# A hybrid attention, GLA and SwiGLU layer on one core: the order of GLA, merge, norm and FFN work changed

## The reference

```python
h = rmsnorm(x, norm_mix_pre)
(a_q, a_kc, ..., mg) = split(h @ w_in)
o_a = nsa_mixer(...)    # compressed, selected and window attention, 8 heads
o_b = gla_mixer(...)    # gated linear attention, 4 heads
o_c = moba_mixer(...)   # block attention, 8 heads
g = sigmoid(mg).reshape(b, s, 3, D_MODEL)
merged = g[:, :, 0] * (o_a @ w_branch_a) + g[:, :, 1] * (o_b @ w_branch_b) + g[:, :, 2] * (o_c @ w_branch_c)
x = x + rmsnorm(merged @ w_out, norm_mix_post)
h = rmsnorm(x, norm_ffn_pre)
gate, up = split(h @ w_ffn_in)
x = x + rmsnorm((silu(gate) * up) @ w_ffn_out, norm_ffn_post)
```

## Time and profile before

| | us |
|---|---|
| three executions | 1012.82, 1013.41, 1020.36 |
| median | 1013.41 |
| the profiled execution | 1015.79 |
| its span, first to last instruction | 1014.1 |
| TensorE busy in the span | 962.9 |
| mean granted TensorE clock | 0.977 |

### The profile page before, as it was taken

One profiled execution on the slowest core, in us unless ns is written; L12 is line 12 of the kernel. 1 busy time (PEld: TensorE's weight loads), 2 busy tenths in 40 slices (PEclk: granted clock), 3 DMA queues, 4 the chain that ended last, 5 costly groups with the idle time before them and its releaser, 6 DMA issues.

```text
span 1014.1 us, 13017 instructions
## 1 busy us (share of the span) xinstructions
PE 962.9 (95%) x4708; PEld 803.2 (79%) x4708; DVE 461.1 (45%) x863; ACT 404.0 (40%) x724; POOL 196.8 (19%) x182
## 2 busy tenths in 40 slices
PE   5999989989899999999989998999999999899994
PEld 3787878878688788788868887988888888788883
DVE  6246655250445555556657747422222222233335
ACT  4333434332446565667754435222222222223322
POOL 4333233333223243234420001000000000000001
PEclk9899979999989999999989999999999999999998
DMA  5178214422232322355365533122332222222312
GB/s 222 64 113 175 75 63 125 146 83 79 78 110 68 104 75 92 105 169 190 110 241 198 171 128 103 42 79 87 103 100 86 103 98 88 83 95 91 103 62 83
DMA packets 37883, 111.37 MB, mean 110 GB/s; under 512 B 4100, under 2 KB 8644, under 8 KB 37324
## 3 DMA queue, kind: packets, MB, share of 16 engines
q1 hardware_dynamic: 37692, 110.49, 33.9%
q10 hardware_dynamic: 144, 0.26, 0.1%
HBM read 93.93 MB, written 13.66 MB: 106 GB/s over the span
## 4 chain that ended last, share of the span: by engine, by line
PE 87%; DVE 5%; DMA 3%; ACT 2%; issue 2%; POOL 1%; POOLq 0%; SPq 0%; ACTq 0%; DVEq 0%
PE bank L1499 25%; PE bank L1500 24%; PE bank L1501 24%; DMA w_raw<-wpack 3%; PE bank L599 3%; PE bank L591 2%; PE bank L613 1%; PE bank L590 1%; PE bank L611 1%; ACT w_hi L841 1%; PE bank L617 1%; PE bank L1515 1%; PE bank L1648 1%; PE bank L1535 1%; DMA xs<-x_in 1%
## 5 line engine op out<-in xcount | busy, mean ns | idle before, releaser
L1499 PE MATMUL bank<-h_hi,w_lo 128*128 128x512 f32 (+1 forms) x680 | 271.1, 399 | 4.4 <-DVE cqs L1228 3.0
L1500 PE MATMUL bank<-h_lo,w_hi 128*128 128x512 f32 (+1 forms) x680 | 266.8, 392 | 0.0
L1501 PE MATMUL bank<-h_hi,w_hi 128*128 128x512 f32 (+1 forms) x680 | 266.7, 392 | 0.0
L1499 PEld LDWEIGHTS bank<-h_hi,w_lo 128*128 128x128 f32 (+1 forms) x680 | 128.6, 189 | 36.9 <-issue 11.4
L841 ACT ACTIVATE w_hi<-w_raw 128x1024 fp32r<-128x1024 f32 (+1 forms) x85 | 89.3, 1051 | 160.4 <-PE bank L1501 152.1
L1501 PEld LDWEIGHTS bank<-h_hi,w_hi 128*128 128x128 f32 (+1 forms) x680 | 128.3, 189 | 28.2
L1500 PEld LDWEIGHTS bank<-h_lo,w_hi 128*128 128x128 f32 (+1 forms) x680 | 128.8, 189 | 23.8
L777 POOL TENSOR_TENSOR w_lo<-w_raw,w_hi 128x1024 fp32r<-128x1024 f32 (+1 forms) x37 | 88.3, 2388 | 153.1 <-ACT w_hi L841 153.1
L1031 ACT ACTIVATE w_hi<-w_raw 128x1024 fp32r<-128x1024 f32 x40 | 42.5, 1063 | 168.8 <-PE bank L1501 168.8
L784 POOL TENSOR_TENSOR sc<-sc,ast 128x512 f32<-128x512 f32 (+1 forms) x96 | 66.3, 722 | 145.0 <-DVE ast L531 111.1
L1441 DVE TENSOR_TENSOR w_lo<-w_raw,w_hi 128x1024 fp32r<-128x1024 f32 x40 | 49.0, 1226 | 90.9 <-ACT w_hi L1031 90.9
(11 more groups left out here) (276 smaller groups left out, 1559.8 us busy)
## 6 DMA issues: line engine op xcount, KB each, us to landing
w_raw<-wpack SPq DMA_DIRECT2D x146, 512.0 KB, 3.3
gate_logits<-gl_out SPq DMA_DIRECT2D x24, 256.0 KB, 2.1
gl_in<-gate_logits SPq DMA_DIRECT2D x24, 256.0 KB, 3.5
near_bias<-near SPq DMA_DIRECT2D x1, 3072.0 KB, 33.8
xs<-x_in SPq DMA_DIRECT2D x4, 512.0 KB, 5.8
fullb<-near_bias SPq DMA_DIRECT2D x16, 128.0 KB, 2.6
ckx<-cks SPq DMA_DIRECT2D x16, 128.0 KB, 2.4
ob<-gla_out SPq DMA_DIRECT2D x2, 1024.0 KB, 7.1
```

The source lines that it names most:

```text
L1499: mm(out, ll, rh, start=start, stop=False, skip_group_check=True)
L1500: mm(out, lh, rl, start=False, stop=False, skip_group_check=True)
L1501: return mm(out, lh, rh, start=False, stop=stop, skip_group_check=True)
```

## The change

- Start: the gate transposes move behind chunk 2, z behind chunk 1, bT behind 3, the levels behind 5 to 11 and the diagonal behind 12. TensorE goes from chunk 0 straight to chunk 1.
- GLA: kd, qb and a state of three tiles get their own memory. Keys and queries are decayed at chunks 5 to 9, the states made at 10 to 12 in banks 4 and 5, the outputs at 13 to 16 in banks 0 to 3. POOL clears the state.
- The compressed softmax is cut in two; its second half comes on VectorE after the next chunk's eviction.
- Attention: TensorE's wait for the last two ck evictions moves from ahead of step 0 to step 8.
- Merge: products are reordered (`PRODUCTS`: branches a and b of n = 0 to 2 first, then their c), use six banks, and the first four are done in halves in steps 96 to 103. Weight splits run one chunk further ahead. A third mrg buffer.
- Output projection: its wait for all 24 products stands ahead of the third tile of its first chunk.
- Norms: VectorE multiplies by the norm weight as it reads PSUM (`weighted`, `z_weight`), before the rstd is there; one fused pass then scales and adds. `transposed_lo(0)` and `(1)` now stand behind `residual(2)` and `(3)`.
- FFN: the first two activation splits come within the last two tiles of the up stage; the down stage starts with the halves in banks 4 to 7. At the end `z_full` counts halves, and the last tile is stored in two halves, the second from ScalarE's queue.

The core of the diff:

```diff
+PRODUCTS = ([(0, 0), (0, 1), (1, 0), (1, 1), (2, 0), (2, 1), (0, 2), (1, 2), (2, 2)]
+            + [(n, b) for n in range(3, KD) for b in range(3)])
+PRODUCT_BANKS = (0, 1, 6, 7, 2, 3)
+ADDS_BEFORE = [sum(b > 0 for _, b in PRODUCTS[:s]) for s in range(N_GATES)]
...
-AUX = (["gates", "z0", "z1", "bT0", "bT1"] + [f"lv{l}_{t}" for l in range(7) for t in range(2)] + ["lv7"]
-       + ["kd0", "kd1", "o0", "s0", "o1", "s1", "o2", "s2", "o3", "cmp", "cbias"])
+AUX = (["z0", "z1", "gates", "bT0", "bT1"] + [f"lv{l}_{t}" for l in range(7) for t in range(2)]
+       + ["lv7", "cmp", "cbias"])
+C_O = STRAIGHT.index(("kc", 0))
...
-        state = at(204, "state", [P, 2, 256])
+        kd = at(112, "kd", [P, 1024])
+        qb = at(116, "qb", [P, 1024])
+        state = at(120, "state", [P, 3, 2, 256])
...
@@ -451,12 +461,13 @@
                     if n < 7:
                         sa.wait_ge(s_full, head_units(n + 1)[1] + 1)
                     sa.activation(hi_, part, ACT.Copy).then_inc(head_hi, 1)
-                if u % 4 == 1 and 0 <= u // 4 - 1 < N_GATES:
+                if u % 4 == 1 and 0 <= u // 4 - 1 < N_GATES + 2:
                     f = u // 4 - 1
-                    sa.wait_ge(w_used, C_GATE + f + 1)
-                    if f >= 2:
-                        sa.wait_ge(gl_stored[f % 2], 16 * (f // 2))
-                    sa.activation(gl_out[:, f % 2, :], gate_bank(f)[:, :], ACT.Copy).then_inc(gl_copied, 1)
+                    if f < N_GATES:
+                        sa.wait_ge(w_used, C_GATE + f + 1)
+                        if f >= 2:
+                            sa.wait_ge(gl_stored[f % 2], 16 * (f // 2))
+                        sa.activation(gl_out[:, f % 2, :], gate_bank(f)[:, :], ACT.Copy).then_inc(gl_copied, 1)
                     hi(C_GATE + f + 2)
 
         def transposed_lo(ve, t):
...
+
+        def compressed_probs(ve, link):
+
...
+        def branch_part(te, three, s, ks):
+
+            b = PRODUCTS[s][1]
+            c, part, out = C_BR + s // 2, s % 2, bank[PRODUCT_BANKS[s % 6]]
+            xh, xl = [(oa[:, :, 0, :], oa[:, :, 1, :]), (ob2[:, 0, :, :], ob2[:, 1, :, :]),
+                      (oc[:, :, 0, :], oc[:, :, 1, :])][b]
+            if ks[0] == 0:
+                if part == 0:
+                    te.wait_ge(w_hi, c + 1)
+                    lo_split(te, c)
+                if s == 0:
+                    te.wait_ge(head_lo, 8)
+                if s == 1:
+                    te.wait_ge(ob_back, 32)
+                if s < 2:
+                    te.wait_ge(s_max, len(UNITS) - 1 + s)
+                elif s < 4:
+                    te.wait_ge(gl_copied, N_GATES - 3 + s)
+                elif s < 6:
+                    te.wait_ge(t_lo, len(UNITS))
+                else:
+                    te.wait_ge(d_free, s - 5)
+                if s == 6:
+                    te.wait_ge(head_lo, 16)
+            for k in ks:
+                cols = slice(512 * part + k * P, 512 * part + k * P + P)
+                last = three(out[:, :], wh[:, c % 2, cols], wl[:, c % 2, cols], xh[:, k, :], xl[:, k, :],
+                             k == 0, k == 3)
+            if ks[-1] == 3:
+                last.then_inc(p_full if part == 0 else w_used, 1)
...
-            single_out(te, slot_of("ck", 3))
-            single_out(te, slot_of("ck", 2))
...
+                    if v == 0:
+                        single_out(te, slot_of("ck", 3))
+                        single_out(te, slot_of("ck", 2))
...
+                elif u < len(UNITS) + PV_LAG:
+                    s, half = divmod(u - len(UNITS), 2)
+                    branch_part(te, three, s, (2 * half, 2 * half + 1))
...
-            def load_logits(f):
-                if f >= 4:
-                    sp.wait_ge(d_sig, f - 3)
-                sp.dma_start(gl_in[:, f % 4, :], gate_dram[f, :, :]).then_inc(gl_read[f % 4], 16)
+            def load_logits(s):
+                n, b = PRODUCTS[s]
+                if s >= 4:
+                    sp.wait_ge(d_sig, s - 3)
+                sp.dma_start(gl_in[:, s % 4, :], gate_dram[3 * n + b, :, :]).then_inc(gl_read[s % 4], 16)
...
+                if c == 6:
+
+                    sa.wait_ge(kd_sub, 1)
+                    sa.activation(kd[:, :], kd[:, :], ACT.Exp).then_inc(kd_sub, 1)
+                    sa.activation(qb[:, :], bT[:, :], ACT.Exp).then_inc(kd_sub, 1)
                     sa.activation(ebl[:, :], bT[:, :].rearrange("p (n c) -> p n c", c=P)[:, :, P - 1],
-                                  ACT.Exp).then_inc(ex_ready, 1)
...
+                if c == 5:
+                    b3 = bT[:, :].rearrange("p (n c) -> p n c", c=P)
+                    ve.tensor_tensor(kd[:, :].rearrange("p (n c) -> p n c", c=P),
+                                     b3[:, :, P - 1:P].broadcast_to([P, 8, P]), b3, ALU.subtract).then_inc(kd_sub, 1)
+                if c == 7:
+                    ve.wait_ge(kd_sub, 4)
+                    ve.tensor_tensor(kd[:, :], kd[:, :], gk[:, :], ALU.mult).then_inc(kd_ready, 1)
+                if c == 8:
+                    ve.tensor_tensor(qb[:, :], qb[:, :], gq[:, :], ALU.mult).then_inc(kd_ready, 1)
+                if c == 11:
...
+                if 10 <= c < 13:
+                    t = c - 10
+                    ve.wait_ge(st_full, t + 1)
+                    ve.wait_ge(const_ready, 5)
+                    ps_s = bank[4 + t % 2][:, :].rearrange("p (a n) -> p a n", a=2)
...
-                if s % 2 == 0 and s > 0:
-                    hi(C_BR + s // 2 + 1)
+                if s % 2 == 0 and s >= 4:
+                    hi(C_BR + s // 2 + 2)
...
-                sa.wait_ge(z_full, t + 1)
                 for half in range(2):
+                    sa.wait_ge(z_full, 2 * t + half + 1)
                     if t + half > 0:
                         sa.wait_ge(z_sq, 2 * t + half)
                     sa.activation(junk[:, :], bank[4 * half + t][:, :], ACT.Square,
                                   accum_out=stat[:, 56 + 2 * t + half:57 + 2 * t + half]).then_inc(z_sq, 1)
+            sa.wait_ge(out_ready, NT + 1)
+            sa.dma_start(out_d[0, (NT - 1) * P:NT * P, 512:1024], x1[:, NT - 1, 512:1024]).then_inc(stored, 16)
...
+            def weighted(t, half):
+                ve.wait_ge(y_sq, 2 * t + half + 1)
+                cols = slice(512 * half, 512 * half + 512)
+                ve.tensor_tensor(x1[:, t, cols], bank[4 * (1 - half) + t][:, :], wpost[:, cols], ALU.mult).then_inc(y_weighted, 1)
+
             def residual(t):
 
                 ve.wait_ge(y_rstd, t + 1)
-                for half in range(2):
-                    ins = ve.scalar_tensor_tensor(out=x1[:, t, 512 * half:512 * half + 512],
-                                                  in0=bank[4 * (1 - half) + t][:, :], scalar=stat[:, 8 + t:9 + t],
-                                                  in1=wpost[:, 512 * half:512 * half + 512], op0=ALU.mult,
-                                                  op1=ALU.mult)
-                link(ins)
-                ve.tensor_tensor(x1[:, t, :], x1[:, t, :], xr[:, t, :], ALU.add).then_inc(x1_ready, 1)
+                ve.wait_ge(y_weighted, 2 * t + 2)
+                ve.scalar_tensor_tensor(out=x1[:, t, :], in0=x1[:, t, :], scalar=stat[:, 8 + t:9 + t],
+                                        in1=xr[:, t, :], op0=ALU.mult, op1=ALU.add).then_inc(x1_ready, 1)
...
-            for t in range(2):
+            weighted(0, 0)
+            for t in range(NT):
                 y_mean(t)
+                weighted(t, 1)
                 residual(t)
-                lo(C_FIN + 2 + t)
+                if t < 2:
+                    lo(C_FIN + 2 + t)
+                else:
+                    transposed_lo(ve, t - 2)
                 x_mean(t)
+                if t + 1 < NT:
+                    weighted(t + 1, 0)
                 normalised(t)
-            transposed_lo(ve, 0)
-            y_mean(2)
-            residual(2)
-            transposed_lo(ve, 1)
-            x_mean(2)
-            normalised(2)
-            y_mean(3)
-            residual(3)
             lo(C_FIN + 4)
-            x_mean(3)
-            normalised(3)
             transposed_lo(ve, 2)
             transposed_lo(ve, 3)
             lo(C_FIN + 5)
@@ -1433,7 +1489,7 @@
                 ve.wait_ge(w_used, C_FIN + 2 * f + 2)
                 ve.tensor_tensor(act[:, f, :], silu[:, f, :], bank[4 * f + 1][:, :], ALU.mult).then_inc(f_free, 1)
 
...
+            for f in range(NF - 2, NF):
+                hi(C_FIN + 2 * f + 2)
+                act_hi(f - NF + 2)
+                sa.wait_ge(w_used, C_FIN + 2 * f + 1)
+                sa.wait_ge(f_free, f + 1)
+                sa.activation(silu[:, f % 2, :], bank[2 * (f % 2)][:, :], ACT.Silu).then_inc(f_sig, 1)
+                hi(C_FIN + 2 * f + 3)
+            for k in range(2, 4):
...
+            def z_weight(t, half):
+                ve.wait_ge(z_sq, 2 * t + half + 1)
+                cols = slice(512 * half, 512 * half + 512)
```

(54 more changed lines are left out.)

297 lines of the change are left out of this document (142 added, 155 removed).

## The result

The changed kernel took 989.46 us (median of four runs, 986.35 to 993.73), the kernel before 1013.29 beside it: ratio 0.9727, interval [0.9681, 0.9774]. A second measurement on another chip gave 990.5 against 1018.29, ratio 0.9748 [0.9712, 0.9785]. The prediction was 985.4, range 975 to 998, with 0.93 on faster by over 1%. The profiled execution is the one of 986.35 us, span 984.6, where the working gave 987.8.

The account below looks back on a forecast made before the run. TensorE, busy 95% of the span, was taken to bound the kernel through its written order: work, stops and half clock. Gains and losses summed to 28.0 us, from 1015.79 to 987.8, or 985.4 against the median; range 975 to 998.

Parts of the forecast that it names:

- Gates (A): Kernel start: the 2.46 us stop for ScalarE's first copy and 3.15 of slow clock go, 0.6 charged; +5.0 us.
- The stop at 95 us: TensorE's wait for a w_raw transfer queued behind the 3 MB bias table, then splits and products; 0.5 left, +1.9 us.
- GLA (B): GLA stretch: stops of 3.0 (zz) and 1.22 us (gr) and 6.4 of slow clock go; +10.6 us, bounds 4.2 to 10.6.
- Compressed softmax: VectorE evicts the cq chunk before waiting for the exponential, so TensorE's stop there goes; +3.0 us.
- Start of attention (D): The 3.66 us wait for ck evictions becomes 2.15 at step 2, 1.5 charged for clock; +2.9 us, bounds 1.0 to 4.4.
- End of attention, merge (E): Stops of 3.7 and 3.25 of clock go; new 4.1 us stop at chunk C_BR+4, 2.0 for clock; net +0.9 us.
- End of merge: First output chunk's third tile waits for all products, with VectorE's split and products behind the last; -1.9 us, bound 0.
- Residual (F): Residual loop: h_lo pieces come later, stop 5.4 us in place of 2.14, 1.7 of clock as before; -2.8, bounds +1.5, -4.5.
- Up to down (G): FFN, up to down stage: early activation splits remove the as_lo stop, 3.2 plus 1.3 us of clock; +4.5 us.
- Last w_lo: FFN down stage: the 3.03 us stop for the last w_lo stays untouched, as both last chunks are waited for together.
- Tail: VectorE's work after TensorE ends at 1007.4 instead of 1011.03, last transfer 0.3 less; +3.9 us, 0.9 lower by another reading.
- six of nine cases: Clock rule: a TensorE stop costs itself and, in six of nine cases, 1.3 to 3.3 us more at half clock.

Follow-up runs that it names:

- p1: Kernel before with only the change's first part (head of the weight stream, early exponentials, GLA states and outputs in own banks): ratio 0.9848.
- u1: Changed kernel with four repairs to its order, but VectorE's compressed softmax in one call again: 977.76 us, ratio 0.9599 to the kernel before.
- e5: Changed kernel with four repairs to its order, plus the second compression layer's two products one weight chunk later: 972.51 us, ratio 0.9551 to the kernel before.
- e2: Changed kernel, its first output projection chunk waiting only for the product that last had each of banks 6 and 7: 985.52 us, ratio 0.9702.
- e1: Changed kernel with residual input and two norm rows issued between the weight chunks of branch products 2 to 7, not as one block: 985.89 us, 0.9684.
- p3: Kernel before with only the change's third part, the FFN and the norms: ratio 0.9947.

## Why the prediction was right

The mechanism held: the written order of TensorE is the time, and every stop that was to go went. Sizes were off in several steps, most in the clock. What each step was worth, from the profiled execution of before to that of after:

- **Gates (A)**, predicted +5.0: stop 2.46 and slow stretch 3.15 gone, the charged 0.6 at the first level came as 0.48 (0.28 became 0.76). 5.1. Right.
- **The stop at 95 us**, predicted +1.9: mis-sized. 0.5 was to be left, 1.42 was. TensorE was there at 92.4 and not at 92.9, and its operand came at 93.8, behind the 92.5 to 93.6 that were given. From ScalarE's split to the last product it took 5.5 us before and after, so the chain was right and the times of arrival were off. Gain 1.0.
- **GLA (B)**, predicted +10.6: the zz and gr rows are gone and the window 130 to 148 reads 1.00. With the two slow stretches read apart that is 3.0 + 1.22 + 6.8 = 11.0. p1's 1.52% (15.5 us) stands against 17.1 for these first three, but its own profile lost 6.2 us in slow stretches that the changed kernel's doesn't have, so this agreement proves little.
- **Compressed softmax**, predicted +3.0: cqs gone; u1 brought back 3.0 plus clock.
- **Start of attention (D)**, predicted +2.9: the stop was 2.14 at step 2, as worked out (2.15). Of the 1.5 charged for the clock nothing was lost in the profiled execution, so 1.5 + 2.9 = 4.4, the upper bound. e5's execution lost 4.72 x 0.34 = 1.6 behind the very same stop, so the charge was a fair mean.
- **End of attention, merge (E)**, predicted +0.9: the new stop stands where it was put, at 3.06 instead of 4.1. TensorE came at +12.4 (predicted +12.3) after the last P.V product, the logits at +12.5 instead of +13.5. The over-sized term is the landing, taken from the burst of before. Net 3.74 + 3.25 - 3.06 - 1.7 = 2.2.
- **End of merge**, predicted -1.9: 1.89, and e2 shows that it was a wait for product 24 where 21 would do.
- **Residual (F)**, predicted -2.8: the stop is 4.73, below the 5.4, but the clock term failed. "1.7 of clock as before" became 2.9 (in e1's execution, behind the same 4.73 us, 6.71 x 0.23 = 1.5). Net 2.14 + 0.41 - 4.73 + 1.7 - 2.9 = -3.4.
- **Up to down (G)**, predicted +4.5: the as_lo row and its stretch are gone. Right.
- **Last w_lo**: the prediction left it at nothing. The stop stayed at 3.03, but the clock fell behind it this time: 1.7. Not foreseen.
- **Tail**, predicted +3.9: 4.3. POOL's power took 0.55 for all four tiles, once right beside the weighting, here in the changed kernel:

```profile
979.59 0.68 DVE L1543 TENSOR_TENSOR xn<-bank,wfpost 128x512 f32<-128x512 f32 x1
```

```profile
979.75 0.55 POOL L879 TENSOR_TENSOR stat<-stat,minus_half 128x1 f32<-128x1 f32 x1 [2.16 <-DVE stat L1537]
```

Neither was held up. In the kernel before, the power of 1.46 us at 1006.74 lay over an add with both inputs in SBUF:

```profile
1006.57 1.21 DVE L1490 TENSOR_TENSOR x<-x,xn 128x1024 f32<-128x1024 f32 x1
```

That is the case for which the prediction quoted the Trainium skill, "SBUF — State Buffer" (SBUF: two separate sides): the lock is between a GpSimd operation that reads SBUF and a VectorE operation with two inputs from SBUF. The trace agrees, by these few rows alone.

These sum to 5.1 + 1.0 + 11.0 + 3.0 + 4.4 + 2.2 - 1.9 - 3.4 + 4.5 - 1.7 + 4.3 = 28.5 against 28.0 predicted and 29.5 between the spans. The misses are of both signs and cancel, which is luck in the sum. So is some of the early third. The prediction read its stops and slow stretches off one execution of before; p3 has the same code up to 590 us, and in its execution the stop at 95 us was 6.05 and not 2.43, with 6.08 x 0.46 = 2.8 us lost behind it (100 to 107.5) where the profile before lost nothing. The prediction's rule for the clock was miscounted too: its "six of nine cases" with "1.3 to 3.3 us" takes B's two stops as one and leaves out the 1.55 us stop for ghid, behind which the clock held. Counted stop by stop from the first copy on it was seven of eleven, with 1.3 to 5.2 us.

In the medians the gain was 23.8 us on the first chip and 27.8 on the second. The first median came out 4 us above the forecast because the profiled execution, at clock 0.992, is the fastest of four. The working was scaled to the median by the execution of before, which stood 2.4 above its own. That correction had the wrong sign for the kernel after, and nothing of before could tell.

## What to carry to other kernels

Read a one-engine-bound kernel as three sums: stops, what the clock loses behind them, and the tail; here removing 11.4 us of stops gave 24.1 with the clock. Where a new order makes a buffer wait for "all of them", count which one last used that buffer: 1.9 us. Ask what is queued behind each bulk transfer (3.1 us), and in an engine's written order, which operation that the bound engine waits for stands behind ones that can wait (4.2 us); but measure where the burst goes instead, since moving one cost 14.
